# A fused hybrid layer on one core: the adaptive-norm products of c with w_ada, in plain fp32 on four column groups

## The reference, cut to what matters

```python
def _hybrid_layer(x, c, w_ada, b_ada, g_norm, w_in, ..., w_out):
    mod = jax.nn.silu(c) @ w_ada + b_ada            # [1, 6144], fp32
    shift, scale, gate = jnp.split(mod, 3, axis=-1)
    h = _rms_norm(x, g_norm) * (1.0 + scale[:, None, :]) + shift[:, None, :]
    proj = h @ w_in                                  # q, k, v, z of two attentions, and an index head
    ...                                              # DSA attention (8 heads), MoBA attention (8 heads)
    y = jnp.concatenate([ya, yb], axis=-1) @ w_out
    return x + gate[:, None, :] * y
```

## Time and profile before

| | us |
|---|---|
| median of 3 runs | 2208.85 |
| lowest, highest of these | 2207.95, 2215.11 |
| span of the profiled execution, first to last instruction | 2204.3 |
| what lies around the span (median less span) | 4.55 |

### The profile page before, as it was taken

The page is one execution under the profiler, slowest core; times in us unless marked ns, Lnnn a source line. Parts: engine busy times, 40 slices in busy tenths (PEclk is TensorE's granted clock), DMA queues, the critical chain, the costliest instruction groups (busy, mean ns, idle before and its releaser), DMA issues.

```text
span 2204.3 us, 30450 instructions
## 1 busy us (share of the span) xinstructions
PE 2086.6 (95%) x11383; PEld 1786.7 (81%) x11383; DVE 1077.0 (49%) x1237; ACT 912.8 (41%) x1177; POOL 1492.3 (68%) x745
## 2 busy tenths in 40 slices
PE   6979999999897989999899999989999999999997
PEld 5667788888786778897799996878888888888886
DVE  6964860151234255626655553037745664752233
ACT  5654444444573443344511114444443344443333
POOL 6975888888796959882411105859988889954442
PEclk9989999999999999999999999999999999999999
DMA  7953555555573635553000003545555555555553
GB/s 271 306 190 134 165 182 190 195 183 190 182 237 125 197 116 181 174 168 119 3 1 0 0 0 136 194 151 191 190 190 190 190 190 190 190 189 184 183 188 133
DMA packets 179984, 352.07 MB, mean 160 GB/s; under 512 B 6175, under 2 KB 18861, under 8 KB 179405
## 3 DMA queue, kind: packets, MB, share of 16 engines
q1 hardware_dynamic: 179021, 346.94, 48.0%
q10 hardware_dynamic: 896, 4.20, 0.5%
HBM read 349.02 MB, written 2.10 MB: 159 GB/s over the span
## 4 chain that ended last, share of the span: by engine, by line
PE 53%; POOL 27%; issue 17%; DVE 2%; ACT 1%; POOLq 0%; DVEq 0%; ACTq 0%
POOL WL L528 26%; PE bank L858 18%; PE bank L860 9%; PE bank L1100 8%; PE bank L814 4%; PE bank L812 4%; PE bank L813 4%; PE bank L1063 1%; PE bank L1073 1%; DVE arena L1941 0%; PE bank L1111 0%; POOLq L527 0%; PE bank L381 0%; POOL HX L783 0%; DVE arena L2098 0%
## 5 line engine op out<-in xcount | busy, mean ns | idle before, releaser
L528 POOL TENSOR_TENSOR WL<-WR,WH 128x1024 fp32r<-128x1024 f32 (+2 forms) x574 | 1405.1, 2460 | 426.7 <-ACT WH L1269 424.5
L1269 ACT ACTIVATE WH<-WR 128x1024 fp32r<-128x1024 f32 (+2 forms) x650 | 678.8, 1049 | 909.2 <-PE bank L814 511.3
L858 PE MATMUL bank<-HX,WH 128*128 128x512 f32 x1840 | 642.5, 396 | 5.6 <-POOL WL L528 4.7
L860 PE MATMUL bank<-HX,WL 128*128 128x256 f32 x1840 | 512.2, 278 | 0.0
L858 PEld LDWEIGHTS bank<-HX,WH 128*128 128x128 f32 x1840 | 345.7, 188 | 87.4 <-issue 5.6
L860 PEld LDWEIGHTS bank<-HX,WL 128*128 128x128 f32 x1840 | 346.4, 188 | 0.0
L812 PE MATMUL bank<-WH,HX 128*128 128x512 f32 (+2 forms) x864 | 334.0, 387 | 10.2 <-DVE HX L1612 7.6
L813 PE MATMUL bank<-WL,HX 128*128 128x512 f32 (+2 forms) x864 | 332.0, 384 | 0.0
L814 PE MATMUL bank<-WH,HX 128*128 128x512 f32 (+2 forms) x864 | 332.0, 384 | 0.0
L528 DVE TENSOR_TENSOR WL<-WR,WH 128x1024 fp32r<-128x1024 f32 x76 | 142.2, 1887 | 177.9 <-ACT WH L1269 176.7
L812 PEld LDWEIGHTS bank<-WH,HX 128*128 128x128 f32 x864 | 163.3, 189 | 41.0 <-DVE HX L1612 7.8
(11 more groups left out here) (315 smaller groups left out, 2468.0 us busy)
## 6 DMA issues: line engine op xcount, KB each, us to landing
WR<-in_w_in SPq DMA_DIRECT2D x97, 1024.0 KB, 5.0
WR<-in_w_ada SPq DMA_DIRECT2D x48, 1024.0 KB, 5.2
WR<-in_ffn_w_gate SPq DMA_DIRECT2D x44, 1024.0 KB, 5.1
WR<-in_ffn_w_up SPq DMA_DIRECT2D x44, 1024.0 KB, 5.1
WR<-in_ffn_w_down SPq DMA_DIRECT2D x44, 1024.0 KB, 5.1
WR<-in_w_out SPq DMA_DIRECT2D x32, 1024.0 KB, 5.1
WR<-in_w_in SPq DMA_DIRECT2D x12, 768.0 KB, 4.4
WR<-in_mla_w_ukv SPq DMA_DIRECT2D x4, 1024.0 KB, 5.6
```

What stands on the lines that cost most here:

```text
L528: eng.tensor_tensor(half(WL, n % NSLOT, *w), half(WR, n % NSLOT, *w), half(WH, nth(n) % 2, *w), ALU.subtract).then_inc(ready, 1)
L858: pe.matmul(bank[:, :].rearrange("p (h n) -> p h n", h=2), wh[:, k, o], HX[:, :, kk, :], start=kk == 0, stop=False, skip_group_check=True)
L860: last = pe.matmul(bank[:, 0:L], wl[:, k, o], HX[:, 0, kk, :], start=False, stop=kk == KT - 1, skip_group_check=True)
L1269: act.activation(half(WH, nth(n) % 2, *w), half(WR, n % NSLOT, *w), ACT.Copy).then_inc(hi_ready, 1)
```

## The change

The w_ada products are no longer split into parts. A piece is now one tile of 128 rows of w_ada by 2048 columns (rows of 8 KB, where before they were 2 KB), still 1 MB. c is spread over 32 columns (CW, one DVE copy). For each piece PE does four plain fp32 matmuls of 512 columns, one for each quarter of the 2048 columns; quarter g has a stationary tile of 32 columns and writes PSUM partitions 32g to 32g + 31 of one bank (ada_piece). So 16 pieces give one of the three rows whole, in one bank, and there is no high, no low, and no WH or WL for these 48 pieces.

Scale comes first now, then shift. ACT copies a finished bank to mod_row; PE turns it into columns by four fp32 matmuls with a selection of the identity (mod_cols, moving operand of 4 columns); DVE adds the bias from PSUM. In the attention every head still has one piece beside it. The gate row is copied once, at the last head, to gate_sum, and is spread over the partitions by four fp32 matmuls with one row of ones each (gate_chunk: two before the w_out products, two after their first chunk); DVE adds each from PSUM to the bias row, which the DMA now puts straight into gate_row.

```diff
+            def ada_row(n, k, c0):
+                if n >= NSLOT:
+                    sp.wait_ge(piece_done, n - NSLOT + 1)
+                sp.dma_start(WR[:, n % NSLOT, :], w_ada[k * P:(k + 1) * P, c0:c0 + D]).then_inc(piece_in[n % NSLOT], 16)
...
-            lows(n_ada, n_kw)
             low(n_kw)
-            lows(n_qi, n_wag)
+            lows(n_qi, n_gate)
+            lows(n_wo, n_wag)
...
-            def ada_piece(n, q, bank, more=0):
-
-                wh, wl = view(WH, nth(n + q) % 2, CH), view(WL, (n + q) % NSLOT, CH)
-                for k in range(PK):
-                    kk = q * PK + k
-                    split(n + q, k, more)
-                    last = product(bank, (CSH[:, kk, :], CSL[:, kk, :]), (wh[:, k, :], wl[:, k, :]),
-                                   kk == 0, kk == KT - 1)
-                    done(k, last)
+            def ada_piece(n, k, bank):
+
+                arrived(n)
+                for g in range(4):
+                    o = slice(32 * g, 32 * g + 32)
+                    last = pe.matmul(bank[o, :], CW[:, k, :], WR[:, n % NSLOT, g * CH:(g + 1) * CH], start=k == 0,
+                                     stop=k == KT - 1)
+                last.then_inc(piece_done, 1)
+
+            def mod_cols(m):
+
+                pe.wait_ge(row_took, m + 1)
+                for j in range(4):
+                    last = pe.matmul(BANK[2 + m][:, 4 * j:4 * j + 4], mod_row[:, m, j * P:(j + 1) * P], group_col,
+                                     start=True, stop=True)
+                last.then_inc(mod_cols_ready, 1)
...
-            for j in range(2):
-                ada_chunk(n_ada + PIECES * j, BANK[j][:, :])
+            for k in range(KT // 2):
+                ada_piece(n_ada + k, k, BANK[0])
...
-            with pe.Fori(1, NADA // 2) as i:
-                for j in range(2):
-                    pe.wait_ge(row_took, i * 2 + j - 1)
-                    ada_chunk(n_ada + PIECES * j, BANK[j][:, :], more=i * (2 * PIECES))
+            for k in range(KT // 2, KT):
+                ada_piece(n_ada + k, k, BANK[0])
+            for k in range(KT):
+                ada_piece(n_ada + KT + k, k, BANK[1])
+                if k == 3:
+                    mod_cols(0)
+            mod_cols(1)
...
+            def gate_chunk(g):
+
+                o = slice(32 * g, 32 * g + 1)
+                if g >= 2:
+                    pe.wait_ge(gate_took, g - 1)
+                pe.matmul(BANK[6 + g % 2][:, :], ones[o, :], gate_sum[o, :], start=True, stop=True).then_inc(gate_ready, 1)
...
+            pe.wait_ge(row_took, 3)
+            gate_chunk(0)
+            gate_chunk(1)
...
-            with act.Fori(2, NADA - 1) as i:
-                rest_then_next(0, more=i * PIECES)
-            rest_then_next(n_kw - PIECES)
+            for m in range(2):
+                act.wait_ge(piece_done, n_ada + KT * (m + 1))
+                act.activation(mod_row[:, m, :], BANK[m][:, :], ACT.Copy).then_inc(row_took, 1)
+            high(n_kw)
+            high(n_qi)
...
+            def gate_then_high(h):
+                if h == 2 * HEADS - 1:
+                    act.wait_ge(piece_done, n_gate + KT)
+                    act.activation(gate_sum, BANK[0][:, :], ACT.Copy).then_inc(row_took, 1)
+                if h >= 2 * HEADS - 2:
+                    high(n_wo + h - (2 * HEADS - 2))
...
-            split_c()
+            spread_c()
...
-            own.link(dve.tensor_tensor(gate_row[:, 0:3 * CH], gate_row[:, 0:3 * CH], bgate_row[:, 0:3 * CH], ALU.add))
...
+            def add_gate(g):
+
+                dve.wait_ge(gate_ready, g + 1)
+                o = gate_row[:, g * CH:(g + 1) * CH]
+                dve.tensor_tensor(o, o, BANK[6 + g % 2][:, :], ALU.add).then_inc(gate_took, 1)
```

More of the change, by code:

```diff
@@ L597, in _ @@
                 chunk(n_br, w_in, b * B_COL + j * CH, CH, shift=b * (8 * PIECES) + j * PIECES)
[L598 to L599 removed]
+            for k in range(KT):
+                ada_row(n_gate + k, k, 2 * D)
             with sp.Fori(0, 4) as i:
```

141 lines of the change are left out of this document (60 added, 81 removed).

## The result

The changed kernel takes 2157.2 us (median of 4 runs, 2152.38 to 2161.63), the kernel before, measured beside it, 2211.98 us (4 runs, 2207.95 to 2220.0). The ratio is 0.9744 with an interval of 0.9717 to 0.977: 2.6% or 54.8 us faster. On record was 2154 us, a gain of 55.1. The total came out right. Its terms did not, and most of what follows is about them. In what follows "the changed kernel" without a run's name is the profiled execution of this first measurement.

What follows compares the result with a forecast made beforehand. PE, busy 95% of the span, was taken as the bound, with the first stage's DMA limited by slot turns. Terms 35 + 0 + 4.1 + 14.2 + 3.5 - 1.7 = 55.1 took 2208.85 to 2154 us; range 2132 to 2212.

Steps and rivals of the forecast that it cites:

- First stage: First w_ada products: three transfers in flight, a piece every 2.60 us, end at 97 us; gain 35, bounds 17 and 43.
- the allowance: First stage: 4 us added for parameter loads and PE's transposes, during which only four slots fill.
- What a piece costs: PE's time for one w_ada piece: 1.72 us, between 0.86 and 3.44; heads of 3.59 us, gain 14.2 over sixteen.
- The rival with all four groups at once: w_ada pieces: all column groups overlap, a piece 0.86 us, a head 2.73, total 2139 us; chance 0.20.
- The 0.32 a head: Attention heads: upper end for the two changes between whole array and groups, 2.7 us less gain in all.
- Seam: From the last first-stage product to PE's next work: gain 0, bounds +3 and -6; scaling about 6 us after that product.
- Start of the attention: PE's wait for CSL ahead of the first scores disappears: gain 4.1 us, bounds 3 and 4.2.
- End of the attention: PE starts w_out about 7 us after its last value product instead of 10.45: gain 3.5, bounds 0 and 6.
- Later row matmuls: Two gate row matmuls behind the first w_out chunk, on PE's path: loss 1.7 us.
- DMA at its old pace: First stage: larger rows and more transfers in flight make no difference; it gains 17, total 2172 us; chance 0.12.
- no overlap: w_ada pieces: column groups do not overlap, a piece 3.44 us, a head 5.31, total 2211 us; chance 0.18.
- the clock in the attention: Attention: PE's clock falls to 1.2 GHz, a head 7.03 us, a loss of 40.8, total 2238 us; chance 0.06.

Runs made afterwards that it cites:

- c_before: The kernel before the change, unaltered, measured and profiled once more: 2213.44 us, ratio 1.0006 against itself.
- c_after: The changed kernel, unaltered, measured and profiled once more: 2156.16 us, ratio 0.9754 to the kernel before.
- v_gate: Changed kernel with the gate's row matmuls in pairs behind w_out's chunks 0 and 1, and DVE's split ahead of the gate additions: 2151.04 us, ratio 0.9712.
- e_one_group: Changed kernel with each piece's four matmuls on one column group, from the second piece of each row on: 2215.03 us, ratio 1.0015 to the kernel before.

## Why the prediction was right in the sum and wrong in its terms

- *First stage*: forecast 35, measured 34.4. The mechanism and the pace held (2.49 us a piece against 2.60), and two transfers in flight brought about the old pace back. That it fits within 1 us is partly luck: the pace is 3.7 us better over 34 transfers, and the allowance, put at 4, came to about 8, half of it from 40 to 60 us, where 329 GB/s were moved instead of 412.
- *What a piece costs*: this is **the step that failed**. I took 1.72 us because PE takes its queue in order. It is 0.86, plus 0.13 for the rest that holds both changes between array and groups (my 0.15 was near). Even by that argument the count was short: a piece that stands alone between other products has five steps, 2.15 us, and four only in a run of pieces. Heads 2.85 instead of 3.59; from the first scores to the last value product 48.9 us instead of 78.0, a gain of 29.1 where 14.2 stood in the sum. The rival with all four groups at once had 28, and its mechanism is the one that the runs show; its total of 2139 us, 18 too low, had nearly the same other terms as mine. The mis-sized part is the overlap; the rest of a head was put at 1.72 + 0.15 and measures 1.86 + 0.13.
- The Trainium skill, "TensorE: Matmul & The Clock Gate", Part 3, said that products in different column groups run concurrently; the traces agree and go beyond its 2.38 times for three tiles, 3.44 / 0.86 = 4.0 times for four in a run of pieces, and 3.55 / 0.99 = 3.6 times for a piece alone. I had kept it as a rival with a chance of 0.20, and should have weighed it above an argument on order that no row supported.
- The Trainium skill, "TensorEngine Tiling (Array Packing)", Key Properties, has the engine drain at each change of mode. No run here shows the drain itself; the rest of 0.11 to 0.13 us bounds what two changes cost. The 0.32 a head that I tied to it did not come.
- *Seam*: forecast 0 with bounds of +3 and -6, measured -4.1. The place and the slow steps beside POOL were named, their number was not worked out: three against one before, at about 2.1 us each. The earlier start of the scaling, which should have paid for them, did not come (7.1 us behind the last product against 7.2), because ACT first waits for the second piece of w_in.
- *Start of the attention*: forecast 4.1. From the key chunk's copy to the first scores the two executions differ by 2.5, and c_before and c_after by 4.7. Within the scatter it is right. PE's wait itself fell from 6.31 to 1.27 us, 5.0, a little beyond the bound of 4.2: ACT no longer has a split ahead of its last two copies.
- *End of the attention*: forecast 3.5, measured 2.6; PE began w_out 7.8 us behind its last value product, not 7. With row matmuls and gate additions behind the first chunks (v_gate) it is 5.5. *Later row matmuls*: -1.7 forecast; the gain went from 64.6 to 62.8.
- The terms as measured give 62.8 us, not 55.1. In c_before against c_after 64.7 us are gained up to the split of the RWKV output. What brought the medians back to 54.8 is not in the change: the pace of the feed-forward stage, worth 9 us, which the prediction did not know; and the length of the RWKV stage. From the first wide product to the split it is 542.7 and 548.7 us in the two executions of the kernel before and 551.2, 547.4 and 547.5 in the three of the changed one, and the longest has the lowest granted clock: from 0.87 and 0.83 in two stretches of the shortest to 0.72 and 0.66 in those of the longest, with 0.86 and 0.68 in c_before. That the clock sets the length is not shown by an experiment. On the chip where nine of the ten runs of the kernel before lie at 2217 to 2221 us, the gain is 64.2 us.
- The rivals: DMA at its old pace falls (412 GB/s), no overlap falls (e_one_group measured what it would have been: 2215.03 against my 2211, heads of 5.40 against 5.31), and the clock in the attention stayed at 1.00.

So the total was right by luck: a term that was 15 us too small met a seam of -4 and executions whose later stages took back the rest.

## What to carry to other kernels

A product with a narrow stationary side (32 columns) in plain fp32 was no better than split parts as long as it stood on one column group (ratio 1.0015), and four times cheaper spread over four groups; before costing such a thing, put one experiment on the overlap, since every later term hangs on it. When a stage loses its engine work, ask how many transfers its buffers now keep in flight, and then who meets whom at the seam behind it: moving work on one engine only moved the meeting of DVE and POOL, and a wait that keeps the two apart brought that stretch from 24.8 to 17.6 us. When a total agrees, compare landmarks all the same, and compare them up to the last one that the change touches.

## What the runs showed of the hardware

- Eight fp32 records of 32 x 512 hold PE for 3.55, 1.83 and 0.99 us on one, two and four column groups, and each further piece in a run on four groups adds 0.86, though each record is listed with about 0.6 us; the time that a record shows is not what it costs. What is left over 0.43 us for each record of the fullest group, both changes of groups included, is 0.11 to 0.13 us.
- The granted clock fell to 0.50 (PE at 1.2 GHz all the time) from 60 to 80 us with two transfers in flight, where PE worked 1.93 us of every 3.54, and stayed at 1.00 with one group, where it worked without a gap. The kernel with four groups stood between, 0.63. It cost nothing in the first stage, but PE was still at the lower level for the first products behind it, and again at w_out: 0.50 from 607 to 613 us, behind a wait of 4.3 us, with products 0.43 us apart instead of 0.23.
- DVE's copy and subtraction of 128 x 512 take 0.42 and 0.69 us alone and 2.6 and 2.7 when they start while one of POOL's subtractions (2.4 us) runs, whichever of the two it is; in the changed kernel the slow ones ended 0.3 to 0.6 us behind POOL's. DVE's L1767, which reads a PSUM bank, took 0.68 beside POOL.
- 1 MB transfers reached 297 GB/s with 1.4 in flight, 321 with 1.6 (rows of 2 KB, the others of 8 KB) and 412 with 3.2, and the landing time rose from 4.9 to 8.0 us.
- The same wide products at a granted clock of 1.00 came at 0.1733 or 0.1767 us a record for a whole stage, in five and in nine of 14 profiles, and none of the views read here says why.
